# Norm factors by Ln and Exp on ScalarE instead of scale-and-add, Sqrt and reciprocal, in a two-stack transformer kernel

## The reference, cut to what matters

```python
def _layer_norm(x, g, b):
    xf = x.astype(jnp.float32)
    mu = jnp.mean(xf, -1, keepdims=True)
    var = jnp.mean(jnp.square(xf - mu), -1, keepdims=True)
    return ((xf - mu) * lax.rsqrt(var + EPS)).astype(x.dtype) * g + b

def rms_norm(x, g):
    xf = x.astype(jnp.float32)
    y = xf * lax.rsqrt(jnp.mean(xf * xf, axis=-1, keepdims=True) + EPS)
    return (y * g.astype(jnp.float32)).astype(x.dtype)
```

## Time and profile before

| | |
|---|---|
| median of 3 runs | 2684.57 us (2684.57, 2697.18, 2684.57) |
| the profiled execution's own time | 2689.81 us |
| its span, first to last instruction | 2688.10 us |
| mean granted clock of TensorE | 0.947 |
| busy: TensorE, VectorE, ScalarE | 2462.9 us, 1663.6 us, 968.7 us |
| HBM traffic over the span | 132 GB/s |

### The profile page before, as it was taken

One profiled execution on the slowest core, in us unless ns is written; L12 is line 12 of the kernel. 1 busy time (PEld: TensorE's weight loads), 2 busy tenths in 40 slices (PEclk: granted clock), 3 DMA queues, 4 the chain that ended last, 5 costly groups with the idle time before them and its releaser, 6 DMA issues. The chain is left out here.

```text
span 2688.1 us, 30895 instructions
## 1 busy us (share of the span) xinstructions
PE 2462.9 (92%) x12224; PEld 1963.5 (73%) x12224; DVE 1663.6 (62%) x2640; ACT 968.7 (36%) x1479; POOL 64.2 (2%) x104
## 2 busy tenths in 40 slices
PE   7999999999998999988989988877899999877997
PEld 4878777766766888866569976644688888666897
DVE  6775755435568757767567764775655453585765
ACT  2322312345423222225345443333332232354543
POOL 0000000100001000002000000000000000000000
PEclk8999999999998999998899999967999999888999
DMA  8355444613342443433225642200245433221553
GB/s 317 99 202 188 168 146 178 229 63 126 131 143 104 139 149 141 142 109 122 86 87 180 195 163 81 69 24 1 94 155 189 156 124 97 91 94 48 172 189 126
DMA packets 95802, 357.15 MB, mean 133 GB/s; under 512 B 10969, under 2 KB 11353, under 8 KB 93353
## 3 DMA queue, kind: packets, MB, share of 16 engines
q1 hardware_dynamic: 93082, 339.37, 36.3%
q0 software_dynamic: 2576, 15.82, 1.6%
HBM read 349.90 MB, written 5.24 MB: 132 GB/s over the span
## 5 line engine op out<-in xcount | busy, mean ns | idle before, releaser
L1347 DVE TENSOR_TENSOR w_lo<-raw,w_hi 128x1024 fp32r<-128x1024 f32 (+1 forms) x456 | 543.3, 1209 | 363.6 <-ACT w_hi L879 363.3
L511 PE MATMUL PS<-h_hi,w_hi 128*128 128x512 f32 (+1 forms) x1904 | 666.3, 350 | 84.6 <-DVE h_lo L1833 28.4
L511 PE MATMUL PS<-h_lo,w_hi 128*128 128x512 f32 (+1 forms) x1904 | 658.4, 346 | 0.0
L511 PE MATMUL PS<-h_hi,w_lo 128*128 128x512 f32 (+1 forms) x1904 | 657.8, 346 | 0.0
L879 ACT ACTIVATE w_hi<-raw 128x1024 fp32r<-128x1024 f32 (+1 forms) x456 | 461.0, 1041 | 540.4 <-PE PS L511 532.9
L511 PEld LDWEIGHTS PS<-h_hi,w_hi 128*128 128x128 f32 x1904 | 366.5, 192 | 149.4 <-issue 67.8
L511 PEld LDWEIGHTS PS<-h_hi,w_lo 128*128 128x128 f32 x1904 | 366.5, 192 | 47.8
L511 PEld LDWEIGHTS PS<-h_lo,w_hi 128*128 128x128 f32 x1904 | 367.1, 193 | 45.8 <-issue 0.5
L511 PE MATMUL PS<-hid_hi,w_hi 128*128 128x512 f32 (+1 forms) x864 | 290.5, 336 | 1.7 <-DVE hid_lo L1721 1.7
L511 PE MATMUL PS<-hid_lo,w_hi 128*128 128x512 f32 (+1 forms) x864 | 290.1, 336 | 0.0
L511 PE MATMUL PS<-hid_hi,w_lo 128*128 128x512 f32 (+1 forms) x864 | 290.1, 336 | 0.0
(11 more groups left out here) (314 smaller groups left out, 2910.9 us busy)
## 6 DMA issues: line engine op xcount, KB each, us to landing
raw<-in_weights SPq DMA_DIRECT2D x434, 512.0 KB, 4.6
ada_ring<-in_ada SPq DMA_DIRECT2D x176, 512.0 KB, 3.8
raw<-in_weights SPq DMA_DIRECT2D x22, 384.0 KB, 4.1
qk<-in_ada SPq DMA_DIRECT2D x4, 1024.0 KB, 11.1
xv<-in_ada SPq DMA_DIRECT2D x4, 1024.0 KB, 13.1
m_hi<-h_spill POOLq DMA_DIRECT2D x4, 1024.0 KB, 8.4
wgt<-in_x SPq DMA_DIRECT2D x2, 1024.0 KB, 22.7
h_spill<-h_hi POOLq DMA_DIRECT2D x1, 2048.0 KB, 9.4
```

The source lines that it names most:

```text
L511: mm = pe.matmul(out, a, b, start=(k == 0 and i == 0), stop=(k == ph.k_tiles - 1 and i == 2))
L1347: dve.tensor_tensor(w_lo[:, s, 0:w], raw[:, s, 0:w], w_hi[:, s, 0:w].bitcast(F32), ALU.subtract)\
```

## The change

The factor is computed as exp(-0.5 * ln(sum / count + EPS)). ScalarE reads the sum from PSUM with Ln, whose scale is 1/count and whose bias is a new SBUF column `eps`, and writes the factor's place. A second ACTIVATE, Exp with scale -0.5, works in place. VectorE's scale-and-add and reciprocal are gone. It waits for `rstd` at the place where they stood, and ScalarE raises `var`. The second head norm of each layer puts its factor in `MEAN` instead of `RSTD`, so that it can be written before the first is used.

```diff
+RMS_SUMS = {5: 7, 6: 8, 7: 11, 8: 12}
...
+        eps = sb("eps", [P, 1])
...
-            def root(ap):
-
+            def root(ap, bank, cols, count, xsum=None):
+
+                if xsum:
+                    act.wait_ge(sem("xsum"), xsum)
+                else:
+                    act.wait_ge(sem("sq_used"), nsq_after[nsd[0]])
                 nsd[0] += 1
+                act.activation(ap, PS[:, bank, cols], ACT.Ln, scale=1.0 / count, bias=eps[:]).then_inc(sem("var"), 1)
                 act.wait_ge(sem("var"), nsd[0])
-                act.activation(ap, ap, ACT.Sqrt).then_inc(sem("sd"), 1)
+                act.activation(ap, ap, ACT.Exp, scale=-0.5).then_inc(sem("rstd"), 1)
...
             act.wait_ge(sem("consts_in"), 96)
+            act.wait_ge(sem("eps"), 1)
...
-                    root(RSTD[:, r])
+                    root((RSTD, MEAN)[j][:, r], 5, r, 64)
...
+            dve.memset(eps[:], EPS).then_inc(sem("eps"), 1)
...
-            def rstd(bank, count, cols, dst, added=False):
+            def rstd(added=False):
 
                 nvar[0] += 1
-                if added:
-                    nmean[0] += 1
-                    dve.wait_ge(sem("xsum"), nmean[0])
-                else:
-                    dve.wait_ge(sem("sq_used"), nsq_after[nvar[0] - 1])
-                dve.tensor_scalar(dst, PS[:, bank, cols], 1.0 / count, EPS, ALU.mult, ALU.add).then_inc(sem("var"), 1)
-                dve.wait_ge(sem("sd"), nvar[0])
-                dve.reciprocal(dst, dst).then_inc(sem("dve_chain"), 1)
-                dve.wait_ge(sem("dve_chain"), chained())
+                nmean[0] += added
+                dve.wait_ge(sem("rstd"), nvar[0])
```

More of the change, by code:

```diff
@@ L1063, in ln_squares @@
                     square(X[:, t, r], T if full else CTX)
-                root(RSTD[:, r])
+                root(RSTD[:, r], 5, r, D)
             def layer_norm(n, full, col, n_h):
@@ L1146, in _ @@
             phase("dkr", copy_to(lambda i: kr[:, :]))
-            root(RSTD)
+            root(RSTD, 5, slice(0, T), CTX)
             c_hi(0)
@@ L1154, in _ @@
             phase("ukn", copy_to(lambda i: kn[:, i, :]))
-            root(MEAN[:, 0:CTX])
+            root(MEAN[:, 0:CTX], 5, slice(0, CTX), 3 * P)
             for i in (2, 3, 4):
@@ L1205, in rms @@
                 r = rng(full)
-                root(RSTD[:, r])
+                root(RSTD[:, r], 5, r, D, RMS_SUMS.get(n_h))
                 for t in range(8):
@@ L1246, in z_tile @@
                     if i == 12:
-                        root(RSTD[:, r])
+                        root(RSTD[:, r], 5, r, CTX)
                     if i == 13:
@@ L1333, in _ @@
                 mlp(f"g{l}", full)
-            root(RSTD[:, LAT])
+            root(RSTD[:, LAT], 5, LAT, D, RMS_SUMS[8])
         @block.vector
@@ L1698, in layer_norm @@
                     dve.tensor_tensor(X[:, t, r], X[:, t, r], MEAN[:, r], ALU.subtract).then_inc(sem("xc"), 1)
-                rstd(5, D, r, RSTD[:, r])
+                rstd()
                 for t in range(8):
@@ L1756, in _ @@
             only_split("dkr")
-            rstd(5, CTX, slice(0, T), RSTD)
+            rstd()
             def c_lo(i):
@@ L1771, in _ @@
             only_split("ukn")
-            rstd(5, 3 * P, slice(0, CTX), MEAN[:, 0:CTX])
+            rstd()
             for t in range(3):
@@ L1827, in rms @@
                 r = rng(full)
-                rstd(5, D, r, RSTD[:, r], added=n_h > 4)
+                rstd(n_h > 4)
                 def lo(t):
@@ L1933, in _ @@
                     if g == 6:
-                        rstd(5, CTX, r, RSTD[:, r])
+                        rstd()
                         for j in range(2):
@@ L2039, in _ @@
                 for j in range(2):
-                    rstd(5, 64, r, RSTD[:, r])
+                    rstd()
                     out = y_slot()
-                    dve.scalar_tensor_tensor(out=out, in0=TMP[:, j, r], scalar=small[:, 54:55], in1=RSTD[:, r],
+                    dve.scalar_tensor_tensor(out=out, in0=TMP[:, j, r], scalar=small[:, 54:55], in1=(RSTD, MEAN)[j][:, r],
                                              op0=ALU.mult, op1=ALU.mult).then_inc(sem("y_made"), 1)
@@ L2049, in _ @@
                 mlp(f"g{l}", full, l)
-            rstd(5, D, LAT, RSTD[:, LAT], added=True)
+            rstd(True)
             for t in range(8):
```

## The result

| | before | after |
|---|---|---|
| median of 7 runs each, us | 2684.57 (2681.16 to 2697.18) | 2671.92 (2667.07 to 2677.97) |
| the profiled execution's own time, us | 2689.81 | 2672.38 |
| its span, us | 2688.10 | 2670.7 |
| mean granted clock of TensorE | 0.947 | 0.953 |

The ratio of the times is 0.9939, with a 95% interval of 0.9922 to 0.9955. By this ratio the change saves 16.4 us (12.1 to 20.9), or 0.6% (0.45 to 0.78%). The forecast was 19.2 us less, and 2665.4 us.

The account below looks back on a forecast made before the run. TensorE is busy 92% of the span, so only its waits, such as at norms, can shrink. Place-by-place terms sum to 19.2 us less, taking the 2684.6 us median to 2665.4 us; range 2653 to 2680 us.

Parts of the forecast that it names:

- five wide norms in front of matmuls: 512-column LayerNorms 0 and 1 and RMS norms 4, 5, 6: 2.0 to 2.1 us less each, 10.2 us together.
- dkv: 512-column norm of the latent keys: 1.9 us less, with 0.2 us of lateness from a new table load.
- dq: 256-column norm: Ln and two table loads in line make the factor later, charged in full as 1.4 us lost.
- spatial gates: Factor's first use comes earlier: 1.4 us less in layer 0 (512 columns), 2.4 us less in layer 1 (256 columns).
- conformer norms: Silu, behind its table load, comes 1.5 us earlier in layer 0 (512 columns), 0.7 us later in layer 1 (256).
- head norms: Two norms per attention, in line on ScalarE: 3.2 us less at 512 columns, 0.2 us more at 256.
- The new chain: Ln, table load, Exp and hops: 2.67 us against 4.77 at 512 columns, 2.24 against 2.70 at 256.
- One for one to TensorE: Whatever a factor's chain loses or gains is gained or lost in full wherever TensorE waits behind it.
- The narrow terms that go the other way: 256-column norms predicted to lose: dq 1.4 us, the layer 1 conformer norm 0.7, the layer 1 head norms 0.2.
- the rival's ground: Like gaps restart TensorE at half or full clock: 8 us more gained (chance 0.11) or 6 to 12 given back (0.25).
- The rival of a dearer table change: Each of 27 table loads in line costs 1.4 us beyond its row: 18.6 us slower, 2703 us; chance 0.05.
- The rival of one load: Exp finds its function in Ln's table, so 19 loads go: 43.9 us less in all, 2641 us; chance 0.01.

Follow-up runs that it names:

- the shifted kernel: The kernel before the change with an unused 4-byte SBUF column at the place of eps; 2689.37 us in 12 runs, ratio 1.000.

## Why the prediction was right, and where it was off

The mechanism, the sign and the places were right. Each term against what the traces show, on the chain itself and in TensorE's gaps:

| term of the sum, us less | predicted | chain | TensorE's gaps |
|---|---|---|---|
| five wide norms in front of matmuls | 10.2 | 2.01 in the first | 10.8 |
| dkv | 1.9 | | 2.1 |
| dq | -1.4 | -1.42 | -1.3 |
| LayerNorms 2 and 3 | 0 | | 0 |
| spatial gates | 1.4 and 2.4 | 1.40 and 2.44 | 1.4 and 2.5 |
| conformer norms | 1.5 and -0.7 | 1.56 and -0.69 | 1.8 and -0.1 |
| head norms | 3.2 and -0.2 | 2.24 and -0.21 | 2.7 and 0 |
| RMS 7 and final | 0.9 | 0.46 in the final | 0.9 |
| sum | 19.2 | | 20.8 |

- *The new chain* held to 0.01 us: Ln at 0.687, the load at 1.283 with a gap of 0.01 to 0.02, Exp at 0.629, the hops. The step that paid was to price Ln by the nearest row with the same operands, Identity from PSUM with a column.
- *One for one to TensorE* held at LayerNorms 0 and 1 and RMS 4 (2.02 each). RMS 6 gave 2.6 and not 2.1. The other 0.5 us are the clock: the sum's last product took 1.06 us at half clock (0.50 granted) before and 0.59 at full clock after. Here it is with the product ahead of it, before and then after:

```profile
2302.18 1.78 PE L550 MATMUL PS<-xv,ones 128*128 128x512 f32 x2 [3.25 <-DVE xv L1664]
```

```profile
2279.37 1.10 PE L554 MATMUL PS<-xv,ones 128*128 128x512 f32 x2 [3.25 <-DVE xv L1668]
```

With `eps` in `small` this product is at half clock at RMS 5 and 6 both, and the gaps there are 6.64 and 6.71 for 6.17 and 6.24, with the same chain.
- *The narrow terms that go the other way* were there on ScalarE with sign and size. The experiment with the narrow norms alone (ratio 0.9996) agrees with a sum near nothing.
- *The spatial gate of layer 1* was priced at 2.4 us from one trace of before, and gave 2.44 there. Part of that is luck: the 1.24 us by which the old stretch is shorter in the shifted kernel (4.72 for 5.97) belong to where the weight splits fell, and against that trace the change gives 1.2 us.
- *The head norms of layer 0* were mis-sized: 3.2 us predicted, 2.24 on the chain. The line was put down as what ScalarE has to run. The sum that the second Ln waits for was left out. TensorE makes it in 2.05 us after 3.33 us of idle time, and the Ln comes 0.93 us behind its load. In the narrow layer 1 this sum hides, and -0.2 was right.
- *The conformer norm of layer 1* cost 0.69 us on ScalarE, as charged, and 0.1 in TensorE's gaps. The same gaps differ by 2.8 us between traces with the old norms (11.05 and 8.25), so what of the 0.69 us reaches TensorE is not shown.
- *The sum against the total*: 20.8 us at the gaps, 17.4 in the span, 16.4 by the ratio. The prediction had no term for a program in which a new tensor moves the others. In the profiled pair the program after is 5.5 us ahead at the first norm and loses 11.5 us in two 256 wide stages. Not all of that is the shift: without it the changed kernel is 2.0 us ahead at the first norm and still loses 3.5 us in the feed-forward behind LayerNorm 2, while the 7.4 us of the last MLP are gone. The shift by itself left the total where it was, so the exact split between it and the run to run scatter (the medians of before and after rest on runs 16 and 11 us apart) is not settled.
- *The clock.* The prediction read RMS norm 5 wrongly. Its row of 1943 to 1948 us in the earlier trace rows begins 5.5 us behind the restart at 1937.49. At the restart itself the granted clock is 0.50, as behind LayerNorm 0, and it is so in both kernels. The first 3 us behind RMS norm 5, before and after:

```profile
1937.50:1940.50 3.00, 3.00 (x6) 1.63 (x6) 3.00 (x9) 1.65 (x4) 0.00 (x0) 0.50 0.01 3
```

```profile
1914.70:1917.70 3.00, 3.00 (x6) 1.61 (x6) 3.00 (x9) 1.66 (x4) 0.00 (x0) 0.50 0.00 0
```

So the rival's ground, that gaps of like length have both outcomes, was not in these rows. All five wide norms in front of matmuls restart at half clock in both traces. The time at half clock behind the five restarts is 29.2 us before and 28.4 after, so there the clock gave next to nothing. Over all stretches of work the time at half clock fell from 136.1 to 122.6 us, which at half pace would be some 7 us of gain (an estimate). The kernel before with the unused column has 125.3 us with the old norms, so this is not shown to come from the change.
- *The rival of a dearer table change* falls: with one load more at each root most of the gaps grow by the row's own length, not by 2.7 us. *The rival of one load* was not what the change does, and the same edit with the set named gives what it priced: 24.7 us more were worked out, 26 to 30 measured, with the loads ahead of ten of the Ln gone as well.

## What to carry to other kernels

Price a factor's chain by its fixed part and its part per element. A table load costs 1.28 us whether the tile has 256 or 512 columns, and a float32 reciprocal on VectorE costs 1.75 or 3.35, so the same rewrite takes 2.1 us off the chain at one width and 0.46 or nothing at the other, and turns negative where ScalarE is itself the line that others wait for. Before two functions of ScalarE replace one, look in the built order at how many loads they bring: naming the set that holds both was worth more here (26 to 30 us) than the change itself (16 us, or 21 with `eps` in `small`), and a single function more still (37 us). And compare TensorE's gaps at the edited places, not only the totals, since an added tensor can change the pace of stages that the edit never touches. Take more than one trace of the old kernel for it: here two of its gaps differed by 1.3 and 2.8 us between traces with the same norms.

## What the runs showed of the hardware that was not expected

- The distance of two matmuls in a stage that TensorE fills without a break, at full granted clock, changes with where tensors lie in SBUF. With 0, 4, 32 and 64 bytes of shift the last MLP runs at 113.3, 118.3, 118.3 and 120.0 ns, the first mixer's 512 wide output products at 233.3, 228.9, 228.9 and 233.3 ns, and the 512 wide feed-forward and first MLP at 233.3, 233.3, 233.3 and 226.7 ns. In the traces in which their tensors are not shifted the 256 wide stages take 113.3 or 117.8 ns, and which stage has which differs even between kernels with the same tensors at the same places, so the address is not the only cause. With one trace of each kernel it is open whether this goes with the kernel or with the execution.
- A table load in line costs its 1283 ns and a gap of 0.01 to 0.02 us and nothing further at the place. 19 more of them cost some 8 us beyond their length over the whole program, together with 61.6 us more at half the granted clock.
